# Recurrence's tail and the gated projection behind it: weight parts split earlier, first tiles begun before the phase ends

## What is computed

```
def step(S, inp):
    r_t, w_t, k_t, v_t, z_t, b_t = inp
    s_z = jnp.einsum('ghvk,ghk->ghv', S, z_t)
    S = S * w_t[:, :, None, :] + s_z[..., None] * b_t[:, :, None, :] + v_t[..., None] * k_t[:, :, None, :]
    return S, jnp.einsum('ghvk,ghk->ghv', S, r_t)
...
outs.append((_head_norm(yd, gn_g, gn_b) + bonus) * g[:, t0:])
...
return jax.nn.silu(_layernorm(h, ln_g, ln_b))        # the convolution's end
```

## Time and profile before

| | |
|---|---|
| median of the runs | 2987.99 us |
| the profiled execution's own time | 2980.72 us |
| its span, first to last instruction | 2978.5 us |
| mean granted TensorE clock | 0.966 |
| TensorE matmul busy | 2771.8 us (93%) |
| VectorE busy | 1932.2 us (65%) |
| ScalarE busy | 1482.3 us (50%) |

### The profile page before, as it was taken

The page is one execution under the profiler, slowest core; times in us unless marked ns, Lnnn a source line. Parts: engine busy times, 40 slices in busy tenths (PEclk is TensorE's granted clock), DMA queues, the critical chain, the costliest instruction groups (busy, mean ns, idle before and its releaser), DMA issues.

```text
span 2978.5 us, 50806 instructions
## 1 busy us (share of the span) xinstructions
PE 2771.8 (93%) x21394; PEld 2323.2 (78%) x21394; DVE 1932.2 (65%) x2283; ACT 1482.3 (50%) x1757; POOL 64.7 (2%) x44
## 2 busy tenths in 40 slices
PE   6997879999989978789999999999999889998999
PEld 4874766888768768768788787887877779996999
DVE  3355855222453657468888888888887557665665
ACT  3344233212333432357776677767776445454443
POOL 1100000000002000010000000000000000000000
PEclk9998999999999989889999999999999989998999
DMA  7514101222225230069999898989996424541453
GB/s 310 219 57 187 50 2 57 102 96 99 98 73 198 72 149 4 2 270 371 335 366 338 337 365 334 373 336 348 365 347 254 160 99 170 187 157 72 156 184 114
DMA packets 81460, 581.70 MB, mean 195 GB/s; under 512 B 9064, under 2 KB 10736, under 8 KB 11504
## 3 DMA queue, kind: packets, MB, share of 16 engines
q1 hardware_dynamic: 78192, 571.49, 50.9%
q10 hardware_dynamic: 3072, 7.33, 0.7%
HBM read 577.73 MB, written 1.05 MB: 194 GB/s over the span
## 4 chain that ended last, share of the span: by engine, by line
PE 81%; DVE 8%; PEld 4%; ACT 3%; issue 2%; DMA 1%; PEldq 0%; DVEq 0%; ACTq 0%; POOLq 0%; POOL 0%; SPq 0%
PE banks L2404 20%; PE banks L2428 10%; PE banks L2731 9%; PE banks L1028 8%; PE banks L816 8%; PE banks L1054 4%; PE banks L850 3%; PE banks L1471 3%; PE banks L3049 3%; PEld banks L644 2%; PEld banks L1983 2%; DVE ring_split L2581 1%; PE banks L488 1%; DVE x_buf L2570 1%; PE banks L2757 1%
## 5 line engine op out<-in xcount | busy, mean ns | idle before, releaser
L2581 DVE TENSOR_TENSOR ring_split<-ring,arena_split 128x2048 fp32r<-128x2048 f32 x336 | 768.2, 2291 | 91.4 <-ACT arena_split L2509 82.5
L2509 ACT ACTIVATE arena_split<-ring 128x2048 fp32r<-128x2048 f32 x336 | 644.2, 1918 | 52.9 <-PE banks L2428 52.9
L306 DVE TENSOR_TENSOR ring_split<-ring,arena_split 128x2048 fp32r<-128x2048 f32 x144 | 329.8, 2292 | 343.7 <-ACT arena_split L300 343.7
L300 ACT ACTIVATE arena_split<-ring 128x2048 fp32r<-128x2048 f32 x144 | 274.3, 1908 | 101.6 <-PE banks L1028 74.0
L2404 PE MATMUL banks<-arena_split 128*128 128x512 f32 x896 | 300.8, 398 | 11.6 <-DVE ring_split L2581 11.6
L2404 PE MATMUL banks<-arena_split,mix_split 128*128 128x512 f32 x896 | 303.2, 401 | 6.4 <-DVE ring_split L2581 6.4
L2428 PE MATMUL banks<-arena_split 128*128 128x512 f32 x896 | 297.4, 392 | 1.0 <-DVE arena_split L2610 1.0
L2404 PEld LDWEIGHTS banks<-arena_split 128*128 128x128 f32 x896 | 169.0, 189 | 48.9 <-DVE ring_split L2581 13.4
L2404 PEld LDWEIGHTS banks<-arena_split,mix_split 128*128 128x128 f32 x896 | 168.4, 188 | 45.2 <-DVE ring_split L2581 8.3
L2428 PEld LDWEIGHTS banks<-arena_split 128*128 128x128 f32 x896 | 168.2, 188 | 43.5 <-issue 4.4
L816 PE MATMUL banks<-mix_split,ring_split 128*128 128x256 f32 x704 | 199.1, 283 | 0.0
(11 more groups left out here) (392 smaller groups left out, 5478.0 us busy)
## 6 DMA issues: line engine op xcount, KB each, us to landing
ring<-parts SPq DMA_DIRECT2D x541, 1024.0 KB, 4.8
arena<-bias ACTq DMA_DIRECT2D x2, 2048.0 KB, 9.1
x_buf<-xt SPq DMA_DIRECT2D x1, 2048.0 KB, 13.0
constants<-con SPq DMA_DIRECT2D x1, 2026.0 KB, 8.2
out<-x_buf ACTq DMA_DIRECT2D x1, 1024.0 KB, 4.9
arena<-lora ACTq DMA_DIRECT2D x2, 256.0 KB, 3.2
arena<-gate ACTq DMA_DIRECT2D x2, 256.0 KB, 3.5
arena<-sgw ACTq DMA_DIRECT2D x2, 256.0 KB
```

What stands on the lines that cost most here:

```text
L300: act.activation(high[:, m % depth, :], slots[:, n % RING, :], ACT.Copy).then_inc(w_high.h, w_high.one(times))
L306: dve.tensor_tensor(low_slots[:, n % RING, :], slots[:, n % RING, :], high[:, m % high.shape[1], :].bitcast(F32), ALU.subtract).then_inc(w ...
L2509: act.activation(high[:, m % 3, :], slots[:, m % RING, :], ACT.Copy).then_inc(wh_ok.h, 1)
L2581: dve.tensor_tensor(low_slots[:, m % RING, :], slots[:, m % RING, :], high[:, m % 3, :].bitcast(F32), ALU.subtract).then_inc(wl_ok.h, 1)
```

## The change

- The high halves of the weights get a new buffer of four places, at column 18592 of the arena (three places at 12320 before). Its last two places lie behind what the recurrence uses.
- At the end of g = 2 and of g = 3 ScalarE and VectorE split part 0 and part 1 of `w_out`, behind all else that they do in that group.
- In the tail's first half ScalarE and VectorE split the token rows 0 to 3.
- In the tail's second half TensorE does the row tiles 0 to 3 of output tile 0, one triple each behind the first solve, the second solve and the state, and the fourth at the end; then the four of output tile 1. These 8 triples stay in two banks, and the projection goes on with them.
- The root of the convolution's variance moves to the end of the first half on ScalarE; its spread (1699) to the start of the second half on TensorE, ahead of the solves. On VectorE the bonus products and gates now stand ahead of the state of the second half, the last two steps of the convolution's norm behind it.
- In the projection, TensorE weaves the triples of part 1 (rows 0 to 3) and then rows 6 and 7 of parts 0 and 1 between the steps of the norm; then come tiles 4, 6, 5, 7 with rows 0 to 3, 6, 7; and at the end rows 4 and 5 of all eight tiles. Only parts 2 and 3 are split there, and only the token rows 6, 7, 4, 5.
- In both layers; nothing else changes.

The diff, cut to its core:

```diff
+        out_high, out_first = Arena(OUT_AT).take_split(4 * PART, 4), stream["got"]
...
+            def out_terms(t, k):
+
+                if not t and not k:
+                    wh, wl = take_split_part(pe, out_high, out_first, 2)
+                    out_weights[:] = [v3(wh, KT), v3(wl, KT)]
+                if t and not k:
+                    pe.wait_ge(bnV.h, bnV.at("v10"))
+                pe.wait_ge(t_low.h, t_low.at(k + 1))
+                wh, wl = out_weights
+                for i, (w, x) in enumerate(((wh, x_high), (wh, x_low), (wl, x_high))):
+                    pe.matmul(bank((7, 1)[t])[:, 0:n], w[:, k, t * P:(t + 1) * P], x[:, k, c0:T],
+                              start=k == 0 and i == 0, stop=False)
...
                 solve_blocks(NG - 1, j)
+                if j:
+                    out_terms(0, 0)
                 solve(NG - 1, j)
+                if j:
+                    out_terms(0, 1)
...
+            out_terms(0, 3)
+            for k in range(4):
+                out_terms(1, k)
...
                 turned_out("vs", g, 3, 256, VS)
                 fill_act(act, g, "p8")
+                if g >= NG - 2:
+                    split_high(act, out_high, out_first + g - (NG - 2), 2 + g - (NG - 2))
...
                 taps.some(dve, 2)
                 if g == stored:
                     mod.store(dve)
+                if g >= NG - 2:
+                    split_low(dve, out_high, out_first + g - (NG - 2), 2 + g - (NG - 2))
...
+                    for k in range(4):
+                        dve.wait_ge(t_high.h, t_high.at(k + 1))
+                        dve.tensor_tensor(x_low[:, k, c0:T], mixT[:, k, c0:T], x_high[:, k, c0:T].bitcast(F32), ALU.subtract)\
+                            .then_inc(t_low.h, t_low.one())
+                    state(NG - 1, 0)
...
-            both(0, 0)
+            both(1, 0)
             var(0)
-            both(0, 1)
+            both(1, 1)
             var(2)
-            both(0, 2)
+            both(1, 2)
             expand(0)
-            both(0, 3)
+            both(1, 3)
             var(1)
             expand(2)
-            both(1, 0)
-            both(1, 1)
+            both(0, 6)
+            both(1, 6)
             var(3)
             expand(1)
-            both(1, 2)
-            both(1, 3)
+            both(0, 7)
+            both(1, 7)
             expand(3)
-            for p in range(2):
-                both(p, 6)
-                both(p, 7)
-            for t in range(4):
+            for t in (4, 6, 5, 7):
+                pe.wait_ge(V_.h, V_.at(f"g{t - 4}"))
+                for k in rows[:6]:
+                    terms(t, k)
+            for t in range(KT):
                 terms(t, 4)
                 terms(t, 5)
...
             add_bonus(1)
-            row_low(7)
+            split_low(dve, high, first + 2, first_m + 2)
             gain(3)
             gated(3)
             put(1)
             row_low(4)
             row_low(5)
-            split_low(dve, high, first + 2, 2)
+            split_low(dve, high, first + 3, first_m + 3)
```

More of the change, by code:

```diff
@@ L1677, in _ @@
                     mm.then_inc(cvP.h, cvP.one("mean"))
+                else:
+                    pe.wait_ge(cvV.h, cvV.at("inv"))
+                    for b in range(cv_n // P):
+                        mm = pe.matmul(bank(3)[:, b * P:(b + 1) * P], cv_inv[:, b:b + 1].broadcast_to((P, P)), C("ident"),
+                                       start=True, stop=True)
+                    mm.then_inc(cvP.h, cvP.one("inv"))
                 fill_pe(pe, NG, f"rhs{j}")
                 solve_blocks(NG - 1, j)
+                if j:
+                    out_terms(0, 0)
                 solve(NG - 1, j)
+                if j:
+                    out_terms(0, 1)
                 if not j:
@@ L1696, in _ @@
                 else:
[L1697 to L1701, removed]
+                    out_terms(0, 2)
                 fill_pe(pe, NG, f"dx{j}")
@@ L1792, in _ @@
                 fill_act(act, NG, f"y{j}")
+                if not j:
+                    act.wait_ge(cvP.h, cvP.at("var"))
+                    act.activation(cv_root[:, 0:cv_n // P], bank(4)[:, 0:cv_n // P], ACT.Sqrt, bias=eps(EPS_LN))\
+                        .then_inc(cvA.h, cvA.one("root"))
             for i in range(2):
@@ L1914, in _ @@
                     dve.tensor_tensor(o, o, gg[:, 2 * d + hp, c0:T], ALU.mult).then_inc(bnV.h, bnV.one(f"g{hp}{d}"))
+            dve.wait_ge(cvP.h, cvP.at("inv"))
+            for i in range(2):
+                dve.tensor_tensor(flat(acc[i]), flat(acc[i]), bank(3)[:, 0:cv_n], ALU.mult).then_inc(cvV.h, cvV.one(f"n{i}"))
+            state(NG - 1, 1)
+            for i in range(2):
+                dve.wait_ge(cvV.h, cvV.at(f"n{i}"))
+                dve.tensor_scalar(flat(acc[i]), flat(acc[i]), Q1(l, "cv_g", i), Q1(l, "cv_beta", i), ALU.mult, ALU.add)\
+                    .then_inc(cvV.h, cvV.one(f"g{i}"))
             dve.wait_ge(bnV.h, bnV.at("g11"))
@@ L1917, in recurrence @@
         end_phase()
+        stream["ahead"] = 4
         return Y, gg, bon
@@ L1956, in mean @@
             def mean(q):
-                pe.matmul(bank(4 + q)[:, 0:n], C("head_sum"), Y[:, q, lo:hi], start=True, stop=True).then_inc(P_.h, P_.one(f"m{q}"))
+                pe.matmul(sum_bank(q)[:, 0:n], C("head_sum"), Y[:, q, lo:hi], start=True, stop=True).then_inc(P_.h, P_.one(f"m{q}"))
             def var(q):
@@ L2023, in _ @@
                     stat.sum(pe, 0)
-                stat.sum(pe, t - 3)
+                if t >= 4:
+                    stat.sum(pe, t - 3)
             for k in range(KT - 3, KT):
@@ L2065, in _ @@
             for t in range(KT):
-                if t == 1:
-                    split_high(act, high, first + 3, 3)
                 act.wait_ge(added.h, added.at(t + 1))
@@ L2111, in _ @@
             centre(2)
-            split_low(dve, high, first, 0)
-            row_low(0)
             centre(1)
             centre(3)
-            row_low(1)
+            row_low(6)
             invert(0)
-            row_low(2)
             invert(2)
@@ L2121, in _ @@
             gated(0)
-            row_low(3)
             add_bonus(0)
-            split_low(dve, high, first + 1, 1)
             invert(1)
```

81 lines of the change are left out of this document (38 added, 43 removed).

## The result

The changed kernel takes **2968.81 us** in the median of 5 runs (2963.66 to 2973.24), the kernel before, timed beside it, 2987.99 us (5 runs, 2985.76 to 2992.53). The ratio is 0.9933, with a 95% interval of 0.9922 to 0.9943: 19.2 us less, where 10.5 were predicted. The rival that comes nearest is (a), 2970.7, that of the kept clock.

The account below looks back on a forecast made before the run. TensorE bounds the kernel: its work, waits and clock. Loop +6.4, tail -3.0, projection -8.8, clock -7.1 and +2.0 make -10.5 from 2987.99, so 2977.5 us; 8-in-10 range 2969 to 2985.5.

Parts of the forecast that it names:

- (a): Rival: clock fully kept, TensorE busy to the meeting, loop's stop does nothing; -17.3 us, 2970.7 us; chance 0.12.
- Part 1: Recurrence loop: splits at the end of g = 2 delay g = 3 by 3.1 and 3.3 us; +6.4 us.
- Part 2: Tail: triples fill TensorE's waits and the head means begin earlier, -2.4 and -0.6 us; -3.0 us.
- Part 3: Projection at unchanged clock: eight triples and old waits go, new waits before tiles 4 and 6 come; -8.8 us.
- Part 4: Clock: most half-rate stretches in the projections go, -7.1 us; one new stretch in either loop, +2.0 us; net -5.1.
- everything: Upper bound of the clock term: all half-rate loss in means and projections won back, -11.9 us.
- (b): Rival: projection clock stays as before, with the loop's new half-rate stretches on top; -3.4 us, 2984.6 us; chance 0.15.
- (c): Rival: stop in g = 3 keeps the loop at half rate for the rest of that group; +12.6 us, 3000.6; chance 0.04.
- (d): Rival: the loop's splits are hidden after all, at their lower bounds; -13.2 us, 2974.8 us; chance 0.05.

Follow-up runs that it names:

- e1: The changed kernel with part 0 of the weights split behind g = 3 and part 1 in the tail's first half, none at g = 2; 2962.77 us.
- e6: The kernel before with only the changed kernel's order of root, spread, state and gates in the tail, no split or triple moved; 2979.19 us.
- e4: The changed kernel with parts 2 and 3 of the weights split early, between the norm's first steps in the projection; 2963.68 us.
- e7: The changed kernel with VectorE's split of weight part 2 moved behind the last norm steps and rows; 2973.78 us.
- e10: Repeat of e5, the changed kernel with the edits of e1 and e4, beside the changed kernel itself; 2955.80 us, ratio 0.9888 to before.
- e3: The changed kernel with the five triples that end the tail moved behind the head means; 2974.56 us.
- e8: The kernel before, unchanged, traced a second time; one execution, 2989.88 us.
- e2: The kernel before with five extra unused products at the end of TensorE's tail, nothing left out; 2986.96 us.
- e5: The changed kernel with the edits of e1 and e4 together; 2955.32 us, ratio 0.9905 to before.
- e9: The changed kernel, unchanged, traced a second time; ratio 0.9932 to the kernel before.

## Why the prediction was right in kind and short in size

**Part 1, the splits in the loop** (+6.4, with the +2.0 of part 4 for the clock +8.4): +3.5 and +3.9, together +7.4, stretches included. Right in place and mechanism, and 1.0 too much in size. The reason for 3.1 and 3.3, that the low half can't start before ScalarE's copy and high half, is in the rows: 1.34 and 2.30 us of waiting ahead of VectorE's split. By e1 the whole of it is 6.6, and the difference between the two figures lies in how much layer 0's loop varies. That a stretch of the clock follows the stop was right too, twice. The split behind g = 3 wasn't tried alone. On VectorE it runs from 405.65 to 407.94, 0.9 us past the end of the mean's products (407.06), which the forecast had taken for cover; the spread that hangs on this chain waits 0.37 us on TensorE in layer 0 and 0.74 in layer 1, so it costs these at most.

**Part 2, the tail** (-3.0): -2.7 in layer 0 and -1.5 in layer 1, -4.1 in all. The order alone (e6) gives more, -3.5 and -1.9, since no triples stand in it. The forecast that TensorE is last in layer 0 (within 0.4 us of the means; 0.35) and ScalarE in layer 1 (some 1 us idle; 0.88) holds. What I left out is the half-rate stretch that before has early in its tails: where the changed tail has one (e4, e7, e10, at 412 to 421 us), layer 0's takes 25.0 instead of 23.9 us, so it is worth 1.0. The stretch isn't one of before alone, then, and how much of the tail's 1.1 it explains stays open.

**Part 3, the projection without its clock** (-8.8): the eight triples are gone from it, 5.6 and 2.8. The new waits are 0.64 and 1.36 in layer 0, with 0.42 ahead of the last sum of squares, and 1.66 and 2.13 in layer 1: 6.2 us where I had 7.3. The chains were right (ended by VectorE's low halves, ahead of tiles 4 and 6), each some 0.3 us too long. This term is short by 1.1.

**Part 4, the clock** (-7.1): this is the step that failed. I held that new waits as long as the old ones would bring stretches again, and left 1.7 us of them in layer 0 and 3.1 in layer 1. In the projections there are none, in this trace nor in the second. What half rate cost before is 5.7 in layer 0 (5.95 less 3.70 for the means, 3.4 behind the second wait) and 6.8 in layer 1 (3.44 less 2.00, and 5.4), 12.5 in all: it all came back, 5.4 more than predicted. Of these, 4.8 are the stretches that I left, and 0.6 that the means lost more than the 2.0 and 1.1 I had reckoned. The bound "everything" stood in the text at 11.9. The runs show the two causes apart. The standstill at the meeting makes the means slow (e3), where the tail's short waits haven't done so already (e8, e6), and e2 shows that fast means are worth nothing as long as VectorE is not earlier as well. Standstills in the projection bring stretches behind them (e7, with 6.04 and 4.76 us), and the one at the meeting doesn't bring the later ones (e3 in both layers, e2 in layer 0). My error was to set a wait's length alone against the stretches of before. In the changed kernel waits of 1.36, 1.66 and 2.13 us left the clock up in every trace that has them (the changed kernel's two, e1's, e3's), while in the first trace of before 2.24 and 2.57 us stood ahead of its fall. Why the changed kernel's waits are harmless, the runs don't show.

**The sum.** Clock 5.4, waits 1.1, tail 1.1 and the loop 1.0 make 8.6 us more gain than the 10.5 predicted; the stages show 18.7, 8.2 more. The 0.4 between them is not assigned. The medians give -19.2.

A second, smaller error lies in the base. I took the differences from one execution 7.3 us below the median and applied them to the median. What varies between the executions of before is in part just the clock in these stages, 5.2 of 9.2 us between the two traces. A change that takes the stretches away wins this too.

**The rivals.** (a), the clock kept, is what happened, in the projection; the loop's stop did cost a stretch in both layers. I gave it 0.12, since layer 1 would keep two pauses of 2.0 and 2.4 us; they measured 1.66 and 2.13. (b), the clock as before, is out. (c), a loop at half rate for the rest of g = 3, didn't come: the stretch of the changed kernel ends at 383.00 in layer 0 and 1167.20 in layer 1, and the longest one in a loop, that of e4, lasts from 1164.50 to 1172.00. (d), hidden splits, is out by e1.

**Open** is what decides between a harmless wait and a costly one. A wait of 2.24 us brought a stretch in layer 0 in both traces of before and in e2, none in e6. The wait of 2.52 us ahead of 432.48 in e2 brought none: the clock is full from there to 441.90. In layer 1 of e6 a stretch stands behind a wait of 1.44 us, shorter than those that did nothing in the changed kernel. A stop of 3.44 us in the loop of layer 1 brought one in four traces of five (in e3 the 64 blocks behind it take 2.08 us, in the changed kernel 3.36). And waits of 0.99 and 1.02 us, 1.7 us apart, are followed by a stretch in two traces of three (e4, e10, not e5), in which layer 1's projection takes 34.8 and 35.1 us instead of 33.4. Length alone doesn't tell, and no run here separates it from what ran before the wait.

## What to carry to other kernels

Look for TensorE's standstills (in these stages those of 2.5 us and more have half rate behind them in all but two cases, shorter ones in some) and read from the windows whether the clock is at half behind them. Such a standstill costs twice, the wait and the slow work behind it; useful work moved into it (here five triples of the next stage) wins both. Put extra work of the other engines where they wait for TensorE, never between two steps that TensorE waits for: the same split cost 2.7 and 3.9 us in the loop and at most 0.5 in the tail (e1). And filling a standstill with idle work buys nothing if another engine sets the end (e2). Take more than one profiled execution as the base of an estimate: two of the kernel before differ by 5.2 us in these stages alone.

## What the runs showed of the hardware

- A half-rate stretch ends under the same kind of work under which it ran: in the changed kernel at 383.00, among the 64 x 64 blocks, in e4 at 421.00. Some are much longer: in the second trace of before TensorE is busy without a pause from 444.24 to 455.00, at 0.52.
- Some come without any standstill: some 10 us into layer 0's tail (408 in before, 410 in its second trace, 412 in e10, 414 in e7, 417 in e4), and about the start of layer 1's (1181 in e1, 1178 in e5, 1186 in e9, 1191 in e4). They come in some executions only. Layer 0's tail is 1.0 us longer with one (25.0 for 23.9), layer 1's 0.5 (19.3 for 18.8).
- An execution's time goes with how much of this it draws: the two traces of before have a mean granted clock of 0.966 and 0.957 with spans of 2978.5 and 2987.7 us, those of the changed kernel 0.968 and 0.969 with 2966.7 and 2964.8.
